# x loaded in column halves by row block, with the second halves behind the first four weight k tiles

## The reference

```python
h = rmsnorm(x, g_mix[l])                       # 256 x 1024
proj = jnp.einsum('bsd,de->bse', h, w_in[l])   # 1024 x 4256
qa, ka, va, cq, ckv, kr, gate_a, gate_b = jnp.split(proj, offsets, axis=-1)
...                                            # MoBA and MLA attention, gates, output projections
x = x + jnp.einsum('bsd,de->bse', g_a * y_a + g_b * y_b, w_out[l])
h2 = rmsnorm(x, g_mlp[l])
u = jax.nn.relu(jnp.einsum('bsd,df->bsf', h2, w_ff1[l]))
x = x + jnp.einsum('bsf,fd->bsd', u * u, w_ff2[l])
return rmsnorm(x, g_final)
```

## Time and profile before

| | us |
|---|---|
| median of 3 runs (range) | 365.75 (365.65 to 366.27) |
| the profiled execution's own time | 365.75 |
| its span, first to last instruction | 363.9 |
| time around the span | 1.85 |
| PE busy | 356.8 (98%) |
| DVE / ACT / POOL busy | 286.9 / 231.5 / 39.9 |
| DMA | 76.77 MB, mean 211 GB/s |

### The profile page before, as it was taken

The page is one execution under the profiler, slowest core; times in us unless marked ns, Lnnn a source line. Parts: engine busy times, 40 slices in busy tenths (PEclk is TensorE's granted clock), DMA queues, the critical chain, the costliest instruction groups (busy, mean ns, idle before and its releaser), DMA issues.

```text
span 363.9 us, 5561 instructions
## 1 busy us (share of the span) xinstructions
PE 356.8 (98%) x2113; PEld 311.6 (86%) x2113; DVE 286.9 (79%) x401; ACT 231.5 (64%) x381; POOL 39.9 (11%) x61
## 2 busy tenths in 40 slices
PE   8999999999999999999999999999999999999993
PEld 7998889887788888888888899999999999999983
DVE  3887972958977777587487879999899988998584
ACT  4996445987565675064366656877677777665424
POOL 2321000000000100000021011111111111310002
PEclk9999999999999999999999999999999999999997
DMA  7998567664331366329164999899999999953003
GB/s 269 389 385 289 227 177 234 225 229 149 136 140 45 114 231 229 115 73 331 59 205 171 250 346 215 277 288 284 311 269 254 274 294 287 286 148 115 2 0 115
DMA packets 42053, 76.77 MB, mean 211 GB/s; under 512 B 1907, under 2 KB 19328, under 8 KB 41776
## 3 DMA queue, kind: packets, MB, share of 16 engines
q1 hardware_dynamic: 37696, 66.59, 53.0%
q0 software_dynamic: 4176, 9.64, 13.5%
q10 hardware_dynamic: 160, 0.27, 0.2%
HBM read 75.44 MB, written 1.05 MB: 210 GB/s over the span
## 4 chain that ended last, share of the span: by engine, by line
PE 96%; DMA 1%; DVE 0%; POOL 0%; issue 0%; SPq 0%; POOLq 0%; ACT 0%; DVEq 0%
PE ps L1397 29%; PE ps L1399 29%; PE ps L1398 29%; PE ps L1404 4%; PE ps L1560 2%; PE ps L1585 2%; DMA raw<-in_w_in_dram 1%; PE ps L1477 0%; POOL qkT_b L520 0%; DVE xs L1152 0%; POOLq L127 0%; DVE wlo L995 0%; ACT whi L533 0%; DVE qkT_b L1387 0%; SPq L364 0%
## 5 line engine op out<-in xcount | busy, mean ns | idle before, releaser
L533 ACT ACTIVATE whi<-raw 128x1024 fp32r<-128x1024 f32 (+4 forms) x125 | 119.5, 1001 | 18.2 <-PE ps L1399 13.3
L924 DVE TENSOR_TENSOR wlo<-raw,whi 128x1024 fp32r<-128x1024 f32 (+3 forms) x66 | 71.8, 1124 | 25.2 <-ACT whi L533 24.9
L1397 PE MATMUL ps<-whi,xT_hi 128*128 128x512 f32 (+2 forms) x192 | 75.2, 391 | 0.4 <-DVE wlo L995 0.4
L1399 PE MATMUL ps<-whi,xT_lo 128*128 128x512 f32 (+2 forms) x192 | 72.7, 378 | 0.0
L1398 PE MATMUL ps<-wlo,xT_hi 128*128 128x512 f32 (+2 forms) x192 | 72.5, 377 | 0.0
L1399 PE MATMUL ps<-xT_hi,wlo 128*128 128x256 f32 x224 | 63.4, 283 | 0.0
L1398 PE MATMUL ps<-xT_lo,whi 128*128 128x256 f32 x224 | 63.4, 283 | 0.0
L1397 PE MATMUL ps<-xT_hi,whi 128*128 128x256 f32 x224 | 63.3, 283 | 0.0
L1397 PE MATMUL ps<-whi,lat_hi 128*128 128x512 f32 (+2 forms) x134 | 51.7, 386 | 0.0
L1398 PE MATMUL ps<-wlo,lat_hi 128*128 128x512 f32 (+2 forms) x134 | 51.2, 382 | 0.0
L1399 PE MATMUL ps<-whi,lat_lo 128*128 128x512 f32 (+2 forms) x134 | 51.1, 382 | 0.0
(11 more groups left out here) (151 smaller groups left out, 489.9 us busy)
## 6 DMA issues: line engine op xcount, KB each, us to landing
raw<-in_w_ff_dram SPq DMA_DIRECT2D x32, 1024.0 KB, 7.1
raw<-in_w_in_dram SPq DMA_DIRECT2D x14, 1024.0 KB, 6.6
raw<-in_w_out_dram SPq DMA_DIRECT2D x4, 1024.0 KB, 5.0
t_raw<-in_w_ff_dram SPq DMA_DIRECT2D x12, 256.0 KB, 8.0
raw<-in_w_ff_dram POOLq DMA_DIRECT2D x12, 256.0 KB, 4.4
t_raw<-in_w_ff_dram POOLq DMA_DIRECT2D x12, 256.0 KB, 7.1
gates<-in_b_gate_dram POOLq DMA_DIRECT2D x2, 1024.0 KB, 6.1
raw<-in_w_o_a_dram SPq DMA_DIRECT2D x2, 1024.0 KB, 5.0
```

What stands on the lines that cost most here:

```text
L533: return nc.scalar.activation(dst, src, ACT.Copy, scale=scale)
L924: nc.vector.tensor_tensor(wlo[:, s, h * w:(h + 1) * w], raw[:, s, h * w:(h + 1) * w], whi[:, s, h * w:(h + 1) * w].bitcast(F32), ALU.subtr ...
L1397: nc.tensor.matmul(dst, a_hi, b_hi, start=start, stop=False)
L1399: return nc.tensor.matmul(dst, a_lo, b_hi, start=False, stop=stop)
```

## The change

SP loads x in three parts (`X_PARTS`): columns 0 to 511 of row block 0 (256 KB), after k tiles 0 to 3 of unit 0 the same columns of row block 1 (256 KB), and then columns 512 to 1023 of both (512 KB). The first half of unit 1 comes as two DMAs of one k tile; its second half stays one DMA of two. ACT and DVE split all four k tiles of unit 1 singly, each behind x's tile of the same k; two semaphores, `even_high` and `even_low`, count the even ones. ACT's squares of x (for the RMS norm) trade places with the high parts of units 2 and 3.

```diff
-WARM_UP = 29
-REWARM = 8
+WARM_UP = (18, 5)
+REWARM = (2, 6)
+X_PARTS = ((0, 1, 0, 4), (1, 2, 0, 4), (0, 2, 4, KT))
...
-            def load_x(t):
-                sp.dma_start(xs[:, t, :], x_v[:, t, :]).then_inc(x_landed[t], 16)
+            def load_x(i):
+                t0, t1, k0, k1 = X_PARTS[i]
+                cols = slice(k0 * P, k1 * P)
+                sp.dma_start(xs[:, t0:t1, cols], x_v[:, t0:t1, cols]).then_inc(x_landed[i], 16)
...
             load_x(1)
-            load_first(1, 0, 2, first_landed)
+            load_x(2)
+            load_first(1, 0, 1, first_landed[0])
+            load_first(1, 1, 2, first_landed[1])
             load_first(1, 2, 4, raw_landed[1])
...
-            pool.wait_ge(x_landed[1], 16)
+            pool.wait_ge(x_landed[2], 16)
...
-            high(1, 0)
-            x_high_both(4)
-            x_high_both(5)
-            high(1, 1)
-            x_high_both(6)
-            x_high_both(7)
+            for k in range(4, KT):
+                x_high_both(k)
+                w = slice((k - 4) * Q_RANK, (k - 3) * Q_RANK)
+                if k < 7:
+                    act.wait_ge((first_landed + [raw_landed[1]])[k - 4], 16)
+                if k % 2 == 0:
+                    copy(whi[:, 1, w], raw[:, 1, w]).then_inc(even_high, 1)
+                else:
+                    copy(whi[:, 1, w], raw[:, 1, w]).then_inc(whi_ready, 1)
...
             for t in range(TT):
+                high_unit(2 + t)
                 squares(xs[:, t, :], D, N_MIX + t, rows[:, 2 * t:2 * t + 2, :].rearrange("p a b -> p (a b)"))
-                high_unit(2 + t)
...
+            highs(0)
+            keep_busy(REWARM[1], 1)
+            highs(1)
+            lows(0)
+            highs(2)
+            lows(1)
+            highs(3)
+            lows(2)
             pe.wait_ge(x_landed[1], 16)
             for k in range(4):
                 turn_x(1, k).then_inc(x_turned, 1)
-            first_rows(0, 3)
-            turn_both(4)
+            lows(3)
             first_rows(1, 0)
             first_rows(1, 1)
-            turn_both(6)
+            pe.wait_ge(x_landed[2], 16)
+            for k in (4, 6):
+                turn_two(0, k)
+                turn_two(1, k).then_inc(x_turned, 1)
             first_rows(1, 2)
             first_rows(1, 3)
```

More of the change, by code:

```diff
@@ L192, in hybrid_block @@
         final_rows = qkT_b[:, 0, :, :].rearrange("p (t a) b -> p t (a b)", t=TT)
-        x_landed = [sem(f"x_landed{t}") for t in range(TT)]
+        x_landed = [sem(f"x_landed{i}") for i in range(len(X_PARTS))]
         gmix_landed = sem("gmix_landed")
@@ L205, in hybrid_block @@
         k_low = sem("k_low")
-        first_landed = sem("first_landed")
+        even_high = sem("even_high")
+        even_low = sem("even_low")
+        first_landed = [sem(f"first_landed{k}") for k in range(2)]
         raw_landed = [sem(f"raw_landed{s}") for s in range(SLOTS)]
@@ L537, in high @@
                 s, w = u % SLOTS, unit_width(u) // 2
[L538 to L540 removed]
+                if h == 0:
                     act.wait_ge(raw_landed[s], 16 * (u // SLOTS + 1))
@@ L628, in _ @@
                 x_high(1, k)
-            high(1, 0)
-            x_high_both(4)
-            x_high_both(5)
-            high(1, 1)
-            x_high_both(6)
-            x_high_both(7)
+            for k in range(4, KT):
[7 more added lines that the diff above has]
+                    copy(whi[:, 1, w], raw[:, 1, w]).then_inc(whi_ready, 1)
+            for i in range(len(X_PARTS)):
+                act.wait_ge(x_landed[i], 16)
             for t in range(TT):
-                act.wait_ge(x_landed[t], 16)
-            for t in range(TT):
+                high_unit(2 + t)
                 squares(xs[:, t, :], D, N_MIX + t, rows[:, 2 * t:2 * t + 2, :].rearrange("p a b -> p (a b)"))
-                high_unit(2 + t)
             high_unit(4)
@@ L1007, in _ @@
                 x_low(1, k)
[L1008 to L1013, removed]
+            for k in range(4, KT):
+                x_low_both(k)
+                w = slice((k - 4) * Q_RANK, (k - 3) * Q_RANK)
+                dve.wait_ge(*(even_high, k // 2 - 1) if k % 2 == 0 else (whi_ready, k // 2 + 1))
+                nc.vector.tensor_tensor(wlo[:, 1, w], raw[:, 1, w], whi[:, 1, w].bitcast(F32),
+                                        ALU.subtract).then_inc(even_low if k % 2 == 0 else wlo_ready, 1)
             for u in range(2, 7):
@@ L1416, in proj @@
                     pe.wait_ge(k_low if k < 2 else wlo_ready, k % 2 + 1)
+                elif u == 1:
+                    pe.wait_ge(*(even_low, k // 2 - 1) if k % 2 == 0 else (wlo_ready, k // 2 + 1))
                 elif k % kts == 0:
@@ L1468, in _, with keep_busy @@
             pe.wait_ge(warm_ready, 1)
-            for _ in range(WARM_UP):
-                nc.tensor.matmul(ps[:, 0, 0:P], warm[:, :], warm[:, :], start=True, stop=True)
+            def keep_busy(n, bank=0):
+                for _ in range(n):
+                    nc.tensor.matmul(ps[:, bank, 0:P], warm[:, :], warm[:, :], start=True, stop=True)
+            keep_busy(WARM_UP[0])
             def turn_x(t, k):
@@ L1477, in turn_x, with turn_two @@
                 return nc.tensor.transpose(ps[:, bank, col:col + P], xs[:, t, k * P:(k + 1) * P], ident[:, :])
[L1479 to L1483, removed]
+            def turn_two(t, k0):
+                turn_x(t, k0)
+                return turn_x(t, k0 + 1)
             def first_rows(t, k):
@@ L1491, in _ @@
             nc.tensor.transpose(ps[:, G_BANK, 0:KT], grow[:, :], ident[0:KT, 0:KT]).then_inc(gains_turned, 1)
+            keep_busy(WARM_UP[1])
             pe.wait_ge(x_landed[0], 16)
@@ L1494, in _, with first_part, highs, lows @@
                 turn_x(0, k).then_inc(x_turned, 1)
[L1495 to L1498, removed]
+            keep_busy(REWARM[0])
+            def first_part(k):
+                w = slice(k * Q_RANK, (k + 1) * Q_RANK)
+                return ps[:, 0, 0:Q_RANK], xT_hi[:, k, 0:P], xT_lo[:, k, 0:P], whi[:, 0, w], wlo[:, 0, w]
+            def highs(k):
+                dst, a_hi, _, b_hi, _ = first_part(k)
+                pe.wait_ge(xT_hi_done, TURNED.index((0, k)) + 1)
+                pe.wait_ge(*(k_high[k], 1) if k < 2 else (whi_ready, k - 1))
+                nc.tensor.matmul(dst, a_hi, b_hi, start=(k == 0), stop=False)
+            def lows(k):
+                dst, a_hi, a_lo, b_hi, b_lo = first_part(k)
+                pe.wait_ge(xT_lo_done, TURNED.index((0, k)) + 1)
+                nc.tensor.matmul(dst, a_lo, b_hi, start=False, stop=False)
+                pe.wait_ge(*(k_low, k + 1) if k < 2 else (wlo_ready, k - 1))
+                nc.tensor.matmul(dst, a_hi, b_lo, start=False, stop=False)
+            highs(0)
[6 more added lines that the diff above has]
+            lows(2)
             pe.wait_ge(x_landed[1], 16)
```

## The result

The changed kernel takes 367.13 us (median of 20 runs, 366.47 to 368.39), against 365.75 us before (20 runs beside them): a ratio of 1.0036, interval [1.0028, 1.0044], so 1.4 us slower. The prediction said 365.4, 0.3 us faster, its range ended at 366.3, and it gave 0.08 to anything over 366.48. Direction and size were wrong. The profiled execution took 367.25 us with a span of 365.4, where before had 365.75 and 363.9: 1.5 us more on either count.

A forecast was written before the change was run, and what follows sets the result against it. PE was taken as the bound, with only the ramp to gain. An earlier turn of row block 1, less holes of 0.50 and 0.30, put the mark 0.36 earlier: 365.75 - 0.36 = 365.4 us, range 364.8 to 366.3.

The forecast's parts named there:

- Turn of row block 1: PE's turn of row block 1's x in the ramp, predicted to start at 7.56 where it was 8.48.
- mark: First matmul of the next chunk (288 columns) on PE, predicted at 16.28 where it was 16.64.
- What bounds the kernel: PE works without a pause from 8.48, so earlier work in the ramp moves the end one for one.
- The first turn: PE's first turn of x, predicted near 3.85 where it was 4.38, after a smaller first x DMA and fewer fillers.
- The DMA engines are full, so each lands about 0.71 earlier: Weight k tiles 0 to 3 stand behind 256 KB less; tile 1 lands at 5.01 instead of 5.72.
- two bounds for tile 1: Landing of weight k tile 1: 5.72 if its lateness has another cause, about 4.4 if it follows its neighbour by its bytes.
- tile 1 lands as late as before: Rival, chance 0.12: ACT's chain starts at 5.74, mark at 17.00, 0.36 slower, 366.1 us; the change loses from 5.38 on.
- The first new hole: Before row block 1's first product: 1.27 through ACT and DVE against PE's cover of 0.77, adding a 0.50 wait.
- The second new hole: Before k tile 4: 2.24 through ACT and DVE against PE's cover of 1.94, adding a 0.30 wait.
- The holes don't open: Rival, chance 0.16: both new PE waits are hidden, the mark comes 0.80 earlier, at 15.5, and time is 364.6 us.
- The late clock: Rival, chance 0.10: a late clock; named among the ways to a time over 366.48 us.
- Behind the mark: ACT's later work comes 0.87 later, but 1.6 us of slack before the KA chunk makes it cost nothing.

The follow-up runs named there:

- e15_e7_again: Changed kernel with x in whole rows, own PSUM banks, five more fillers, two turns of each row block put back as cover; a repeat run: 365.54 us, 0.9987.
- e1_own_banks: Changed kernel with k tiles 4 to 7 each in its own PSUM bank and DVE waiting for its own tile only: 366.36 us, 1.0018.
- e3_loads_only: Kernel before with only the changed x loads (three parts) added, engine orders as before: 367.01 us, 1.0033.
- e13_x0_halves_apart: Kernel before with row block 0's x in two column halves, row block 1 whole, POOL's small loads kept behind row block 1: 366.51 us, 1.0020.
- e8_cover: Changed kernel with only row block 0's x in halves, own banks for k tiles 4 and 5, row block 1's turns as cover: 367.00 us, 1.0032.
- e2_whole_rows: Changed kernel with x back in two DMAs of whole rows, engine orders and fillers as changed: 367.92 us, 1.0054.
- e14_orders_x1_halves: Changed kernel's orders with own banks, cover turns and five more fillers, row block 0's x whole and only row block 1's in halves: 365.32 us, 0.9988.
- e10_x0_halves: Kernel before with row block 0's x in two column halves, row block 1 whole; POOL's small loads went out early: 366.84 us, 1.0030.
- e12_k0_first: Kernel before with weight k tile 0 issued ahead of row block 0's x in whole rows: 366.39 us, 1.0021.

## Why the prediction was wrong

Turn of row block 1 to mark, after: 18.18 - 8.64 = 9.54, predicted 8.72. Turn: 8.64, predicted 7.56. The miss at the mark is 1.90 us (18.18 for 16.28): 1.08 in the turn and 0.82 behind it. Against the executions before, the same in other words: the turn is 0.16 later than before, and the way from it to the mark 1.38 longer.

- **What bounds the kernel** was right. In after the time moved one for one with the mark (1.54 and 1.5), and the old order's 7.98 from turn to mark without holes ("8.16 - 0.18") is what `e15_e7_again` shows.
- **The first turn**, predicted at 3.85, stands at 3.72; ACT's first copy at 4.24 for 4.37.
- **"The DMA engines are full, so each lands about 0.71 earlier" is the step that failed**, and it set the turn. K tile 1 landed near 6.02, not 5.01; x's last part near 9.4, not 8.44. In `e1_own_banks`, with the same loads, tile 1 came near 5.2 and tile 2 held the chain in its place (6.9), so what failed is the even shift of all landings and not the reading of one tile. The share of 0.92 was read as a fixed rate, into which fewer bytes ahead could be put. But the share says that engines are occupied, not how fast they move bytes: before and after have 0.98 and 0.95 and 339 and 291 GB/s. What took up the time that the smaller first part should have freed is not shown: it hangs on x's halves (`e3_loads_only`, `e13_x0_halves_apart`), and the length of a row alone does not explain it (391 GB/s with packets under 2 KB). The prediction's two bounds for tile 1 (4.4 and 5.72) both left that out; the landing came 0.3 beyond the worse one. From there on the chain went as worked out: ACT's copies at 6.04, 6.72, 7.38 (period 0.67, predicted 0.66), and the turn 2.60 behind the first of them (2.54 predicted).
- **The rival "tile 1 lands as late as before"** came nearest. It gave 0.12 of the chance and 366.1 us, and its own rule, that the change loses from 5.38 on, held. Its reason was another, late landing for a cause apart from the bytes ahead.
- **The first new hole** was right: 1.12 us from turn to product, for 1.27; a hole appeared where predicted, released by DVE's low part. Its wait is printed as 0.17, counted from the end of the matmul before; counted from starts, as the prediction does, it is about 0.33 for 0.50.
- **The second new hole** failed by 0.78 us. The sum of 2.24 was right for one tile (`e1_own_banks`: 2.26). The step that was missed is the wait for the pair: the diff put a weight copy between the two x copies on ACT, and the code of `x_low_both`, not in the diff, waits for both. That adds one ACT period, 12.35 - 11.57 = 0.78. The prediction asked what ACT and DVE do one behind the other, and not on which count DVE waits.
- **The holes don't open** was wrong in after, since nothing covered them; with two turns of each row block put back as cover and a bank for each tile they vanish (`e15_e7_again`), worth 0.82 against the predicted 0.80.
- **The late clock** (0.10 of the chance) is not what happened in the profiled execution: six fillers from 4.95 took 0.51 us there, where the same six took 0.86 in `e8_cover` (from 5.22). The 0.10 was the author's estimate; no run shows a late rise of the granted clock, which is printed as 1.00 in both. What the runs showed in its place is a long pitch that ends late in some executions: 0.32 us per 384 columns up to 8.57 in `e2_whole_rows`, 0.18 from 6.96 on in after.
- **Behind the mark** nothing came of the 0.87, as said.
- **A sum that is off by little.** 0.73 + 3.3 is 4.03, not 4.07. Nothing hung on it, since PE's fillers set the first turn.

Put together, by the profiled executions from after to the best kernel: the pair wait 0.74 (9.54 to 8.80 from turn to mark), the missing cover 0.88 (8.80 to 7.92), and a turn 0.49 earlier (8.64 to 8.15) with row block 0 in whole rows and five fillers more. That is the 2.11 us between the marks of after and of `e14_orders_x1_halves`. The medians are 1.8 apart; the profiled execution of `e14_orders_x1_halves` was its quickest (365.12 us).

## What to carry to other kernels

When copies are moved on one engine, look up the count that each consumer waits for, also in the code that the diff leaves alone: a wait for a pair turns whatever is put between the two into delay (0.74 us from turn to mark here). A first load in smaller pieces starts the first step earlier but can slow all loads behind it (here 291 GB/s for 339); read the rate in GB/s over the whole ramp, not the busy share. Here halving the later load was free and halving the first was not. A turn or a transpose that looks movable may be the cover for another engine's latency (0.82 to 0.88 us here).

## What the runs showed of the hardware

- A busy share near 1 goes with very different rates: 0.98 of the DMA engines' time moved 339 GB/s with x in whole rows of 4 KB, and 0.98 moved 311 with the first 512 KB in column halves of 2 KB rows (same window, same bytes). Two DMAs of 64 partitions each with whole rows moved 281 at a share of 1.04. Loads with every packet under 2 KB moved 391 at 1.08 (before, 9 to 12 us).
- The moment at which PE's pitch falls to about half (0.32 us per 384 columns to 0.18) moved between profiled executions: about 5.3 us in the kernel before and 8.57 in `e2_whole_rows`; and with nearly the same program up to there, `e10_x0_halves` still had 0.32 us per 384 columns at 9.24 while `e13_x0_halves_apart` had 0.18 at 6.97. The granted clock is printed as 1.00 over all of these stretches, so the pitch has to be read. Between the last two the moment differs by more than 2 us, and why is not shown. It need not cost much: in `e10_x0_halves` row block 1's x came at 9.7 anyway, as in `e13_x0_halves_apart`, and the mark stands 0.29 later (18.18 for 17.89), with its turns at 9.75 still slow (0.66 us to the next product for 0.41).

Open are the reason why the loads are slow behind a first half of row block 0, which the length of its rows alone does not give, and why `e12_k0_first` is slow in its median.
